# Squares of three norms' last tiles added by GpSimd instead of by products with ones, and a table load one instruction later

## The chip, the cores and the metric

The kernel runs on one core of a Trainium2 chip. Its time is device time in microseconds (us), the median of several executions. The engines are TensorE (PE, matrix products; PEld is its weight load), VectorE (DVE), ScalarE (ACT), GpSimd (POOL) and SyncE (SP, which issues the weight DMAs). Each engine runs its own instructions in order, and they wait for each other on counting semaphores.

## What is computed

Two layers of a first transformer block, then one layer of a second one, over 512 tokens and 1024 features. Each sublayer's result goes through an RMS norm before it is added to the residual stream `x`:

```python
def rms_norm(x, gain):
    xf = x.astype(jnp.float32)
    y = xf * lax.rsqrt(jnp.mean(xf * xf, axis=-1, keepdims=True) + RMS_EPS)
    return (y * gain.astype(jnp.float32)).astype(x.dtype)
...
        x = x + rms_norm_2(merged @ w_out[l], g_mix_post[l])
        h = rms_norm_2(x, g_mem_pre[l])
        m = rms_norm_2(mem, g_mem_kv[l])
```

What the change touches is the mean of squares over the 1024 features of three such values: the output projection (`wout`, once in each of the three layers), the gate of the per-layer embedding (`ple`, once in each of the two layers of the first block), and the memory (`mem`, 256 rows, once, in the second block).

## The kernel before

**Layout.** Features lie on the 128 partitions, in 8 tiles of 128 features; tokens lie along a row. So a sum of squares over the features is a sum over tiles and over partitions. The sum over partitions is a product with a matrix of ones on PE: `square_sum` (line 805) and `sum_of` (line 833) multiply a 256-token half of a tile of squares by `ones`, and several such products into one PSUM region also add tiles up. ACT then takes the root (`half_root`, lines 1511 to 1516: a logarithm and an exponential), DVE scales the tile into `sg`, POOL adds `sg` to `x` (line 3107), ACT and DVE split the new `x` into a rounded high and a low part (`h_hi`, `h_lo`, or `raw_x_hi`, `raw_x_lo` for the next layer), and PE multiplies these.

**Order of the sublayer.** Projections of 8 output tiles run tiles 0 to 3 over all 512 tokens, and then `last_units` (line 1079): the last four tiles, two at a time in one PSUM bank, first for tokens 0 to 255 (units 4 and 5 of the count, half 0) and then for tokens 256 to 511 (units 6 and 7, half 1). Between units, each engine's order is written out by hand. PE goes from half 1 of `wout` straight on to the next stage's first products (`first_units`, line 1100), which start on half 0 of the new `x`; from half 1 of `ple` it goes to `begin` (line 860). The norm's whole chain for half 0 has to be done beside PE's products of half 1, and the chain for half 1 beside PE's first products of the next stage.

**Who adds the squares.** ACT squares tiles 0 to 3 into `sq`, POOL adds them into `sq_acc` (a part of the tile `rstd`; line 3102). ACT squares units 4 to 7 too (`half_squares` line 1518, `ple_squares` line 1956). Of each half POOL adds only the first unit (two instructions of 128x256, line 3068); the second unit's two squares go to PE as they are. So each half of `wout` costs PE 3 products (1 of `sq_acc`, 2 of `sq`), half 0 of `ple` 3, and half 1 of `ple` 5 (two more of `res`, where the last unit's squares of that half lie). The memory's 8 squares go to PE one product each (`sum_mem`, lines 1316 to 1319), two behind each of the tiles 4, 6, 8 and 10 of the merge `am`. PE's place for a sum is fixed: behind the second block (k or j = 1) of the unit that follows, for `ple` behind j = 6 (half 0) and k = 5 (half 1).

**DVE beside it.** When ACT has squared a unit, DVE copies it out of PSUM (`half_out`, line 2272). In `wout`, what follows on DVE behind unit 5 is the low part of a weight unit (`w_lo`, `gu_lo` or `mq_lo`, line 2132), and behind unit 7 the tree of additions for the next norm (lines 2265 and 2266). In `ple`, what follows behind unit 7 is line 2132 and then the tree of lines 2190 and 2191.

Of the kernel before, what the change touches and what calls it, by code (L numbers as in the profile page):

```python
# [176 lines left out]
def stage(name, A=0, **more):  # L177
# [16 lines left out]
    stage("wout", A=8, SS=6, AD=7), stage("post1", N=2, X=16),  # L194
    stage("norm2", W=16, SQ=16, Q=2, SS=4, N=2), stage("gu", A=KF, R=KF, G=KF),
    stage("dn", A=8, SS=2, AD=6), stage("post2", N=1, X=8),
    stage("pp"), stage("xple", W=8), stage("ple", A=8, SQ=8, SS=2, AD=5), stage("post3", N=2, X=16),
# [5 lines left out]
    stage("bm2", A=8), stage("am", A=8), stage("normm", R=8, SQ=8, SS=8, N=1),  # L203
    stage("mk"), stage("mv"), stage("dsa", I=32, H=16, O=4), stage("cm", A=8, R=8),
    stage("wout", A=8, SS=6, AD=7), stage("post1", N=2, X=16),
# [74 lines left out]
def block_kernel(nc, stream, xT, pT, memT, vec1, gains, cst, pos, out):  # L280
    with ExitStack() as ctx:
# [418 lines left out]
        def _(pe):  # L700
# [123 lines left out]
            def half_sum(c, st, half):  # L824

                if st == "mo":
                    direct_sum(c, st, half)
                    return
                square_sum(sq_added, c.at("AD", st, 5 + 2 * half), sq_acc[:, cols(half)], True, False, ps=HALF_SS[half])
                for j in range(2):  # L830
                    square_sum(act_took, c.at("A", st, 6 + 2 * half), sq[:, j, cols(half)], False, j == 1, ps=HALF_SS[half])
# [7 lines left out]
            def gate_sum(c, half):  # L839

                pe.wait_ge(sq_added, c.at("AD", "ple", 5))
                pe.wait_ge(sq_ready, c.at("SQ", "ple", 6 + 2 * half))
                last = [sq[:, j, cols(half)] for j in range(2)]
                if half == 1:
                    last += [res[:, 0, cols(j)] for j in range(2)]
                sum_of([sq_acc[:, cols(half)]] + last, half)
# [13 lines left out]
            def begin(c, st, turn):  # L860
# [27 lines left out]
                for half in range(2):  # L888
                    at = cols(half)
                    for i, p in enumerate(in_turn(half)):  # L890
                        if half == 0:
                            pe.wait_ge(lo_ready, c.at("U", st, p + 1))
                        ps = free_bank(c, st, 2 * half + i)
                        hi, lo = home(c, u0 + p)
                        for k in range(KD):
                            if i == 0:
                                pe.wait_ge(raw_split, c.begun("W", KD * half + k + 1))
                            for g in range(2):
                                b = slice((8 * g + k) * P, (8 * g + k + 1) * P)
# [200 lines left out]
            def first_units(c, st, norm_st, before, also=None):  # L1100

                u0 = c.base[st]["U"]
                for half in range(2):
                    at = cols(half)
                    for p in range(2):
# [4 lines left out]
                        for k in range(KD):  # L1110
# [6 lines left out]
                            if half == 0 and p == 0 and k == (KD - 1 if before == "mo" else 1):  # L1117
                                half_sum(c, before, 1)
# [48 lines left out]
            def first_block(L):  # L1167
# [115 lines left out]
                last_units(c, "ple", lambda k, at: h_hi[:, k, at], lambda k, at: h_lo[:, k, at], 6)  # L1283
# [106 lines left out]
        def _(act):  # L1390
# [127 lines left out]
            def half_squares(c, st, n):  # L1518
# [3 lines left out]
                act.wait_ge(sq_added, c.at("AD", st, 3 + two * (2 + 2 * half)))  # L1522
# [83 lines left out]
            def project_norm(c, st, after, which, norm_st):  # L1606
# [14 lines left out]
                half_root(c, st, 0, 3, HALF_RSTD[0][:, 0:HALF])  # L1621
# [5 lines left out]
                half_root(c, st, 1, 6, HALF_RSTD[1][:, 0:HALF])  # L1627
# [209 lines left out]
            def first_block(L):  # L1837
# [127 lines left out]
                ple_gate(5)  # L1965
                log_table()
                ple_squares(5)
# [103 lines left out]
            def norm_mem(m):  # L2071

                if 1 <= m <= 4:
                    for j in range(2 * m - 2, 2 * m):
                        squares(c, "normm", j, memf[:, j, :], (mem_loaded, 16), N_MEM)
                elif m == 5:
                    root("normm", c, KD, N_MEM, D, dst=mem_rstd[:, :])
# [937 lines left out]
        def _(pool):  # L3015
# [47 lines left out]
            def half_squares(c, st, half, ready=act_took, kind="A"):  # L3063

                for j in range(2):
                    pool.wait_ge(ready, c.at(kind, st, 5 + 2 * half))
                    pool.wait_ge(sq_added, c.at("AD", st, 3 + j + 2 * half))
# [28 lines left out]
            def project_norm(c, st, after, ready=act_took, kind="A"):  # L3096
# [361 lines left out]
```

## Time and profile before

| | |
|---|---|
| time, 3 runs | 2672.48 us median (2671.38 to 2672.74) |
| the profiled execution | 2670.99 us, span of its trace 2668.9 us |
| granted TensorE clock | 0.998 of full speed |
| PE busy | 2622.5 us, 98% of the span |
| DVE, ACT, POOL busy | 1720.7, 1310.8, 494.9 us |
| weight load on PE busy | 2268.1 us |
| DMA | 246.55 MB, mean 92 GB/s |

PE is busy nearly all the time, and the other engines have time left; DMA is far from full. Busy time is an average, though. What matters for this change is what each engine does in some twenty stretches of about 5 us, and which of the waits there is the last. A matmul's record is longer than its turn, since matmuls are pipelined: turns are read from start to start.

### The profile page before, as it was taken

The numbers are of one execution on the slowest core, as the hardware profiler recorded it, in microseconds if no ns is written. First come the engines' busy times: TensorE is split into PE (matmuls) and PEld (weight loads), VectorE is DVE, ScalarE is ACT, GpSimd is POOL, SyncE is SP. The second block draws the span as 40 slices with busy tenths as digits, with TensorE's granted clock in tenths as the row PEclk, the third lists the DMA queues.
The fourth block names the chain that finished last, engine by engine and source line by source line (L and its number), as shares of the span: only waits on it lengthen the run. The fifth ranks groups of instructions, "written<-read, shape, count | busy, mean of one in ns | idle before, by whom it ended". The sixth has DMA issues, their size and how long they took to land.

```text
span 2668.9 us, 40629 instructions
## 1 busy us (share of the span) xinstructions
PE 2622.5 (98%) x15848; PEld 2268.1 (85%) x15848; DVE 1720.7 (64%) x2770; ACT 1310.8 (49%) x2297; POOL 494.9 (19%) x515
## 2 busy tenths in 40 slices
PE   8999999999999999999999999999999999999997
PEld 7887778999988988777899998897787689999986
DVE  6767544888624765755389872475689536798743
ACT  6446543555524644654355562463634635555531
POOL 1424001210102311500121010241011012210101
PEclk9999999999999999999999999999999999999999
DMA  4321123223332232111222233222232221123232
GB/s 153 126 95 36 53 79 112 76 89 105 112 110 95 80 127 95 48 56 64 95 94 84 109 111 111 95 95 79 95 111 80 83 101 69 64 95 110 103 120 79
DMA packets 37958, 246.55 MB, mean 92 GB/s; under 512 B 4624, under 2 KB 5648, under 8 KB 8976
## 3 DMA queue, kind: packets, MB, share of 16 engines
q1 hardware_dynamic: 34032, 239.09, 25.3%
q10 hardware_dynamic: 3744, 4.94, 0.5%
q8 instruction: 126, 2.06, 0.3%
q14 instruction: 56, 0.46, 0.1%
HBM read 241.91 MB, written 2.10 MB: 91 GB/s over the span
## 4 chain that ended last, share of the span: by engine, by line
PE 55%; DVE 2%; issue 1%; ACT 1%; POOL 0%; ACTq 0%; POOLq 0%
PE bank L711 13%; PE bank L713 12%; PE bank L712 12%; PE bank L1159 4%; PE bank L1161 4%; PE bank L1160 4%; PE bank L992 1%; PE bank L949 1%; PE bank L808 1%; PE bank L1304 0%; PE bank L970 0%; PE bank L921 0%; ACT w_hi L1415 0%; DVE st_neg L2436 0%; PE bank L1005 0%
## 5 line engine op out<-in xcount | busy, mean ns | idle before, releaser
L2132 DVE TENSOR_TENSOR w_lo<-raw,w_hi 128x2048 fp32r<-128x2048 f32 x129 | 300.4, 2329 | 322.6 <-ACT w_hi L1415 322.1
L711 PE MATMUL bank<-h_hi,w_hi 128*128 128x512 f32 (+1 forms) x1224 | 474.0, 387 | 3.2 <-DVE ob_lo L2698 1.3
L713 PE MATMUL bank<-h_hi,w_lo 128*128 128x512 f32 (+1 forms) x1224 | 464.3, 379 | 0.0
L712 PE MATMUL bank<-h_lo,w_hi 128*128 128x512 f32 (+1 forms) x1224 | 463.7, 379 | 0.0
L1415 ACT ACTIVATE w_hi<-raw 128x2048 fp32r<-128x2048 f32 x148 | 282.3, 1910 | 223.4 <-PE bank L713 213.9
L1159 PE MATMUL bank<-half_hi,w_hi 128*128 128x256 f32 x1344 | 381.0, 283 | 0.0
L1161 PE MATMUL bank<-half_hi,w_lo 128*128 128x256 f32 x1344 | 380.8, 283 | 0.0
L1160 PE MATMUL bank<-half_lo,w_hi 128*128 128x256 f32 x1344 | 380.8, 283 | 0.0
L711 PEld LDWEIGHTS bank<-h_hi,w_hi 128*128 128x128 f32 x1224 | 230.5, 188 | 55.1 <-issue 11.9
L713 PEld LDWEIGHTS bank<-h_hi,w_lo 128*128 128x128 f32 x1224 | 230.4, 188 | 44.0
L712 PEld LDWEIGHTS bank<-h_lo,w_hi 128*128 128x128 f32 x1224 | 230.8, 189 | 39.3
L1159 PEld LDWEIGHTS bank<-half_hi,w_hi 128*128 128x128 f32 x1344 | 258.4, 192 | 0.1
L1160 PEld LDWEIGHTS bank<-half_lo,w_hi 128*128 128x128 f32 x1344 | 258.3, 192 | 0.1
L1161 PEld LDWEIGHTS bank<-half_hi,w_lo 128*128 128x128 f32 x1344 | 258.4, 192 | 0.0
L711 PE MATMUL bank<-a_hi,w_hi 128*128 128x512 f32 x528 | 205.9, 390 | 0.9 <-DVE w_lo L2144 0.9
L712 PE MATMUL bank<-a_lo,w_hi 128*128 128x512 f32 x528 | 205.6, 389 | 0.0
L713 PE MATMUL bank<-a_hi,w_lo 128*128 128x512 f32 x528 | 205.6, 389 | 0.0
L2531 DVE TENSOR_TENSOR w_lo<-raw,w_hi 128x512 fp32r<-128x512 f32 x192 | 141.5, 738 | 32.5 <-ACT w_hi L1726 31.3
L1669 ACT ACTIVATE pT<-bank 128x512 f32<-128x512 f32 (+3 forms) x160 | 79.7, 498 | 109.5 <-PE bank L949 109.4
L1726 ACT ACTIVATE w_hi<-raw 128x512 fp32r<-128x512 f32 x192 | 118.6, 623 | 17.5 <-PE bank L1161 9.3
L1789 ACT ACTIVATE parts<-bank 128x256 f32<-128x256 f32 x192 | 72.7, 378 | 94.7 <-PE bank L1161 94.6
L711 PEld LDWEIGHTS bank<-a_hi,w_hi 128*128 128x128 f32 x528 | 99.2, 188 | 21.8 <-DVE w_lo L2144 1.5
(510 smaller groups left out, 5749.4 us busy)
## 6 DMA issues: line engine op xcount, KB each, us to landing
raw<-in_stream SPq DMA_DIRECT2D x225, 1024.0 KB, 4.8
x<-in_xT SPq DMA_DIRECT2D x4, 512.0 KB, 9.2
out_T<-x ACTq DMA_DIRECT2D x8, 256.0 KB, 2.1
raw<-in_stream SPq DMA_DIRECT2D x2, 512.0 KB, 7.1
p_f<-in_pT ACTq DMA_DIRECT2D x2, 512.0 KB, 3.6
memf<-in_memT ACTq DMA_DIRECT2D x1, 1024.0 KB, 5.3
cst_sb<-in_cst ACTq DMA_DIRECT2D x1, 409.0 KB, 7.2
pos_i<-in_pos ACTq DMA_DIRECT2D x1, 258.0 KB, 5.4
```

The costliest lines, as they stand in the source:

```text
L711: nc.tensor.matmul(ps, wh, xh, start=start, stop=False)
L712: nc.tensor.matmul(ps, wh, xl, start=False, stop=False)
L713: return nc.tensor.matmul(ps, wl, xh, start=False, stop=stop)
L1159: nc.tensor.matmul(ps, wh[:, b], half_hi[:, i, k, :], start=opens, stop=False, skip_group_check=on)
L1160: nc.tensor.matmul(ps, wh[:, b], half_lo[:, i, k, :], start=False, stop=False, skip_group_check=on)
L1161: mm = nc.tensor.matmul(ps, wl[:, b], half_hi[:, i, k, :], start=False, stop=k == KD // 2 - 1, skip_group_check=on)
L1415: nc.scalar.activation(home(c, v)[0][:, :], raw[v % 2][:, :], ACT.Copy).then_inc(hi_ready, 1)
L1669: nc.scalar.activation(a["pT"][h % 2][:, 0:n, b * P:(b + 1) * P], turned_bank(c, st, i)[:, 0:n * P].rearrange("p (t q) -> p t q", t=n), AC ...
L1726: ins = nc.scalar.activation(factor(c, v, i, w_hi), factor_value(c, v, i), ACT.Copy)
L1789: nc.scalar.activation(parts[:, PIECES[i], :], ps[:, 0:HALF], ACT.Copy).then_inc(piece_taken, 1)
L2132: nc.vector.tensor_tensor(lo[:, :], raw[v % 2][:, :], hi[:, :].bitcast(F32), ALU.subtract).then_inc(lo_ready, 1)
L2531: ins = nc.vector.tensor_tensor(factor(c, v, i, w_lo), factor_value(c, v, i), factor(c, v, i, w_hi).bitcast(F32), ALU.subtract)
```

## The change

It does six things.

- **Units 5 and 7 of `wout`, and unit 5 of `ple`:** their two squares are now added into `sq_acc` by POOL, two more instructions each. Unit 6 of `ple` was in the sum of half 1 as `sq`; POOL adds it now. PE's sum is then one product for each half of `wout` and for half 0 of `ple`, and three for half 1 of `ple`.
- **Places on PE:** the sum of half 0 of `wout` stands behind block 6 instead of 1, that of half 1 behind block 3 instead of 1; in `ple` behind 7 instead of 6 and behind 6 instead of 5.
- **Waits:** each sum waits for POOL's additions alone (half 1 of `ple` also for ACT's last squares).
- **Places on POOL:** the two additions of unit 7 of `wout`, and those of unit 6 of `ple`, stand behind all eight additions to `x` of half 0 and ahead of those of half 1.
- **Table load:** in `ple`, ACT loads the logarithm's table behind the squares of unit 5, not ahead of them.
- **Memory norm:** ACT squares two tiles in one instruction (4 of 128x512 for 8 of 128x256), POOL adds them up (3 of 128x512, 1 of 128x256), and PE makes one product behind tile 10 for eight.

The core of the diff:

```diff
@@ half_sum, on PE
-                square_sum(sq_added, c.at("AD", st, 5 + 2 * half), sq_acc[:, cols(half)], True, False, ps=HALF_SS[half])
-                for j in range(2):
-                    square_sum(act_took, c.at("A", st, 6 + 2 * half), sq[:, j, cols(half)], False, j == 1, ps=HALF_SS[half])
+                square_sum(sq_added, c.at("AD", st, 7 + 4 * half), sq_acc[:, cols(half)], True, True, ps=HALF_SS[half])
@@ gate_sum, on PE
-                pe.wait_ge(sq_added, c.at("AD", "ple", 5))
-                pe.wait_ge(sq_ready, c.at("SQ", "ple", 6 + 2 * half))
-                last = [sq[:, j, cols(half)] for j in range(2)]
+                pe.wait_ge(sq_added, c.at("AD", "ple", 7 + 2 * half))
                 if half == 1:
-                    last += [res[:, 0, cols(j)] for j in range(2)]
-                sum_of([sq_acc[:, cols(half)]] + last, half)
+                    pe.wait_ge(sq_ready, c.at("SQ", "ple", 8))
+                sum_of([sq_acc[:, cols(half)]] + ([res[:, 0, cols(j)] for j in range(2)] if half == 1 else []), half)
@@ places on PE: begin, project, first_units, the gate
-                            if (half, i, k) == (0, 0, 5):
+                            if (half, i, k) == (0, 0, 6):
                                 gate_sum(Counts(BASE1, turn - 1), 1)
...
-                last_units(c, st, hi, lo, 1)
+                last_units(c, st, hi, lo, 6)
...
-                            if half == 0 and p == 0 and k == (KD - 1 if before == "mo" else 1):
+                            if half == 0 and p == 0 and k == (KD - 1 if before == "mo" else 3):
                                 half_sum(c, before, 1)
...
-                last_units(c, "ple", lambda k, at: h_hi[:, k, at], lambda k, at: h_lo[:, k, at], 6)
+                last_units(c, "ple", lambda k, at: h_hi[:, k, at], lambda k, at: h_lo[:, k, at], 7)
@@ sum_mem, on PE
-                for j in range(n - 4, n - 2) if n in (4, 6, 8, 10) else ():
-                    square_sum(sq_ready, c.at("SQ", "normm", j + 1), sq[:, j % 2, 0:N_MEM], j == 0, j == KD - 1)
+                if n == 10:
+                    square_sum(sq_added, c.at("AD", "normm", 4), sq[:, 0, 0:N_MEM], True, True)
@@ the gate, on ACT
                 ple_gate(5)
+                ple_squares(5)
                 log_table()
-                ple_squares(5)
@@ POOL, the norm behind wout and ple
-                half_squares(c, st, 0, ready, kind)
+                half_squares(c, st, 4, 3, ready, kind)
+                half_squares(c, st, 5, 5, ready, kind)
                 for half in range(2):
                     for m in range(KD):
                         pool.wait_ge(post_ready, c.at("X", after, KD * half + m + 1))
                         nc.gpsimd.tensor_tensor(x[:, m, cols(half)], x[:, m, cols(half)], sg[:, m % 2, cols(half)], ALU.add).then_inc(x_ready, 1)
                         if half == 0 and m == 4 and st != "ple":
-                            half_squares(c, st, 1)
+                            half_squares(c, st, 6, 7)
+                    if half == 0 and st == "ple":
+                        half_squares(c, st, 6, 7, ready, kind)
+                    elif half == 0:
+                        half_squares(c, st, 7, 9)
@@ POOL, ahead of norm(c, "normm", 2)
+            for j in range(1, 4):
+                pool.wait_ge(sq_ready, c.at("SQ", "normm", j + 1))
+                if j >= 2:
+                    pool.wait_ge(sq_added, c.at("AD", "normm", j - 1))
+                nc.gpsimd.tensor_tensor(sq[:, 0, :], sq[:, 0, :], sq[:, 1, :], ALU.add).then_inc(sq_added, 1)
+            pool.wait_ge(sq_added, c.at("AD", "normm", 3))
+            nc.gpsimd.tensor_tensor(sq[:, 0, 0:N_MEM], sq[:, 0, 0:N_MEM], sq[:, 0, N_MEM:S], ALU.add).then_inc(sq_added, 1)
```

The order of instructions, which stands in the program and holds no times: first POOL in the norm behind the first layer's `wout`, before. L3102 adds the squares of tiles 0 to 3, L3068 those of the last units, L3107 adds to `x`, L3044 belongs to the feed-forward part.

```order
106 L3018 TENSOR_TENSOR m_lo_125<-res,m_hi_124 128x512 x8
107 L3102 TENSOR_TENSOR rstd<-sq 128x512
108 L3102 TENSOR_TENSOR rstd<-rstd,sq 128x512 x2
109 L3068 TENSOR_TENSOR rstd<-rstd,sq 128x256 x2
110 L3107 TENSOR_TENSOR x<-x,sg 128x256 x5
111 L3068 TENSOR_TENSOR rstd<-rstd,sq 128x256 x2
112 L3107 TENSOR_TENSOR x<-x,sg 128x256 x11
113 L3044 TENSOR_TENSOR a_lo_127<-res,a_hi_126 128x512 x4
```

The same stretch of POOL's order now (L3108 is the addition to `x`):

```order
106 L3017 TENSOR_TENSOR m_lo_125<-res,m_hi_124 128x512 x8
107 L3102 TENSOR_TENSOR rstd<-sq 128x512
108 L3102 TENSOR_TENSOR rstd<-rstd,sq 128x512 x2
109 L3068 TENSOR_TENSOR rstd<-rstd,sq 128x256 x4
110 L3108 TENSOR_TENSOR x<-x,sg 128x256 x5
111 L3068 TENSOR_TENSOR rstd<-rstd,sq 128x256 x2
112 L3108 TENSOR_TENSOR x<-x,sg 128x256 x3
113 L3068 TENSOR_TENSOR rstd<-rstd,sq 128x256 x2
114 L3108 TENSOR_TENSOR x<-x,sg 128x256 x8
```

Four additions of squares stand ahead of the additions to `x` where two stood, and two more stand between those of half 0 and those of half 1.

Second, ACT at the gate of the first layer, before. `res<-bank` takes unit 5 out of PSUM, `sq<-e` squares it, L1515 and L1516 are the root of half 0.

```order
633 L1956 ACTIVATE sq<-e 128x2x256
634 L1436 ACTIVATE res<-bank 128x512
635 L1460 ACT_TABLE_LOAD
636 L1956 ACTIVATE sq<-e 128x2x256
637 L1515 ACTIVATE rstd<-bank 128x256
```

And now (L1456 is the table load, L1952 the squares):

```order
633 L1952 ACTIVATE sq<-e 128x2x256
634 L1432 ACTIVATE res<-bank 128x512
635 L1952 ACTIVATE sq<-e 128x2x256
636 L1456 ACT_TABLE_LOAD
637 L1511 ACTIVATE rstd<-bank 128x256
```

The squares of unit 5 and the table load have changed places; nothing else moved on ACT here. DVE's order is the same before and now over the whole program.

## Rows read from the trace of the kernel before

**Rows 1.** what PE waited for: us in total, times, longest us

```profile
PE bank L711 <- DVE raw_x_lo L2658: 10.9, 1, 10.9
```

**Rows 2.** timeline of PE, first `wout`, half 0: start, us, instruction [idle before <-releaser]

```profile
462.68 0.28 PE L713 MATMUL bank<-m_hi,w_lo 128*128 128x256 f32 x1
462.80 0.60 PE L808 MATMUL bank<-rstd,cst_sb 128*128 128x256 f32 x2
...
464.21 0.28 PE L712 MATMUL bank<-m_lo,w_hi 128*128 128x256 f32 x1
```

**Rows 3.** timeline of PE, first gate, the sums of half 0 and half 1

```profile
875.73 0.28 PE L713 MATMUL bank<-h_hi,w_lo 128*128 128x256 f32 x1
876.28 0.67 PE L836 MATMUL bank<-rstd,cst_sb 128*128 128x256 f32 x2 [0.27 <-ACT sq L1956]
...
877.77 0.28 PE L712 MATMUL bank<-h_lo,w_hi 128*128 128x256 f32 x1
...
890.84 0.28 PE L713 MATMUL bank<-raw_x_hi,second_lo 128*128 128x256 f32 x1
...
893.32 0.28 PE L712 MATMUL bank<-raw_x_lo,second_hi 128*128 128x256 f32 x1
```

**Rows 4.** one line of POOL: duration ns min/median/max, first and last start

```profile
L3068 POOL TENSOR_TENSOR rstd<-rstd,sq x16: 727/782/2327, 457.3 to 2225.0; 128x256 f32<-128x256 f32 x16
```

**Rows 5.** timeline, GpSimd and VectorE at the first gate and ahead of the first `dn`

```profile
869.42 2.29 DVE L2132 TENSOR_TENSOR second_lo<-raw,second_hi 128x2048 fp32r<-128x2048 f32 x1 [1.11 <-ACT second_hi L1415]
...
869.98 2.33 POOL L3068 TENSOR_TENSOR rstd<-rstd,sq 128x256 f32<-128x256 f32 x1 [5.38 <-ACT sq L1956]
...
714.33 5.50 DVE L2481 TENSOR_TENSOR a_lo<-a_val,a_hi 128x512 fp32r<-128x512 f32 x9
720.59 3.65 DVE L2132 TENSOR_TENSOR w_lo<-raw,w_hi 128x2048 fp32r<-128x2048 f32 x1 [0.75 <-ACT w_hi L1415]
...
717.40 4.69 POOL L3210 TENSOR_TENSOR p_lo<-p_f,p_hi 128x1024 fp32r<-128x1024 f32 x1 [10.60 <-ACT p_hi L1929]
```

**Rows 6.** timeline of the first `wout`, half 0, unit 5

```profile
462.34 0.60 ACT L1524 ACTIVATE sq<-bank 128x512 f32<-128x512 f32 x1
464.30 0.39 ACT L1515 ACTIVATE rstd<-bank 128x256 f32<-128x256 f32 x1 [1.36 <-PE bank L808]
...
463.58 2.28 DVE L2132 TENSOR_TENSOR gu_lo<-raw,gu_hi 128x2048 fp32r<-128x2048 f32 x1
```

**Rows 7.** timeline of the same norm, half 1, unit 7

```profile
475.29 0.48 DVE L2258 SCALAR_TENSOR_TENSOR h_lo<-x,vec,h_hi 128x256 fp32r<-128x256 f32 x1 [0.30 <-ACT h_hi L1532]
...
476.68 1.22 DVE L2265 TENSOR_TENSOR sq<-sq 128x1024 f32<-128x1024 f32 x1
...
475.47 0.57 ACT L1524 ACTIVATE sq<-bank 128x512 f32<-128x512 f32 x1
...
476.33 0.60 PE L808 MATMUL bank<-rstd,cst_sb 128*128 128x256 f32 x2
```

**Rows 8.** timeline of the first gate: VectorE in half 0, then half 1, unit 6

```profile
878.69 0.87 DVE L2823 SCALAR_TENSOR_TENSOR sg<-e,vec,bank 128x256 f32<-128x256 f32 x2 [3.77 <-ACT bank L1516]
...
889.13 0.62 ACT L1956 ACTIVATE sq<-e 128x512 f32<-128x512 f32 x1
...
890.08 2.28 DVE L2132 TENSOR_TENSOR w_lo<-raw,w_hi 128x2048 fp32r<-128x2048 f32 x1
892.28 1.21 DVE L2190 TENSOR_TENSOR sq_x<-sq_x 128x1024 f32<-128x1024 f32 x1
```

**Rows 9.** timeline of the memory norm: ACT's last squares, PE's last two products

```profile
2024.88 0.41 ACT L1456 ACTIVATE sq<-memf 128x256 f32<-128x256 f32 x1
...
2033.15 1.02 PE L808 MATMUL bank<-sq,cst_sb 128*128 128x256 f32 x4
```

**Rows 10.** timeline behind the third `wout`: VectorE's first query tile, PE's first score

```profile
2242.54 1.41 DVE L2280 SCALAR_TENSOR_TENSOR mq<-bank,rstd 128x256 f32<-128x256 f32 x4
...
2244.39 0.38 PE L1005 MATMUL bank<-mk,mq 128*128 128x256 f32 x1
```

More of the change, by code:

```diff
@@ L193 @@
     stage("am", A=8), stage("cm", A=8, R=8),
-    stage("wout", A=8, SS=6, AD=7), stage("post1", N=2, X=16),
+    stage("wout", A=8, SS=2, AD=11), stage("post1", N=2, X=16),
     stage("norm2", W=16, SQ=16, Q=2, SS=4, N=2), stage("gu", A=KF, R=KF, G=KF),
     stage("dn", A=8, SS=2, AD=6), stage("post2", N=1, X=8),
-    stage("pp"), stage("xple", W=8), stage("ple", A=8, SQ=8, SS=2, AD=5), stage("post3", N=2, X=16),
+    stage("pp"), stage("xple", W=8), stage("ple", A=8, SQ=8, SS=2, AD=9), stage("post3", N=2, X=16),
     stage("begin", W=16),
@@ L202 @@
     stage("z2", A=9, R=8), stage("lru", A=4, R=4),
-    stage("bm2", A=8), stage("am", A=8), stage("normm", R=8, SQ=8, SS=8, N=1),
+    stage("bm2", A=8), stage("am", A=8), stage("normm", R=8, SQ=4, SS=1, AD=4, N=1),
     stage("mk"), stage("mv"), stage("dsa", I=32, H=16, O=4), stage("cm", A=8, R=8),
-    stage("wout", A=8, SS=6, AD=7), stage("post1", N=2, X=16),
+    stage("wout", A=8, SS=2, AD=11), stage("post1", N=2, X=16),
     stage("normh", W=16, SQ=16, Q=2, SS=4, N=2), stage("mq"), stage("mem", I=16, H=4, O=4),
@@ L1521, in half_squares @@
                 dst = sq[:, :, cols(half)]
-                act.wait_ge(sq_added, c.at("AD", st, 3 + two * (2 + 2 * half)))
+                act.wait_ge(sq_added, c.at("AD", st, 3 + two * (2 + 4 * half)))
                 act.wait_ge(tile_done, c.at("T", st, n + 1))
@@ L1620, in project_norm @@
                 half_squares(c, st, 5)
-                half_root(c, st, 0, 3, HALF_RSTD[0][:, 0:HALF])
+                half_root(c, st, 0, 1, HALF_RSTD[0][:, 0:HALF])
                 for m in range(KD):
@@ L1626, in project_norm @@
                 half_squares(c, st, 7)
-                half_root(c, st, 1, 6, HALF_RSTD[1][:, 0:HALF])
+                half_root(c, st, 1, 2, HALF_RSTD[1][:, 0:HALF])
                 last_half(c, norm_st, which, after, "gu" if norm_st == "norm2" else "mq")
@@ L2073, in norm_mem @@
                 if 1 <= m <= 4:
-                    for j in range(2 * m - 2, 2 * m):
-                        squares(c, "normm", j, memf[:, j, :], (mem_loaded, 16), N_MEM)
+                    act.wait_ge(mem_loaded, 16)
+                    if m >= 3:
+                        act.wait_ge(sq_added, c.at("AD", "normm", m - 2))
+                    nc.scalar.activation(sq[:, min(m - 1, 1), :].rearrange("p (j t) -> p j t", j=2), memf[:, 2 * m - 2:2 * m, :],
+                                         ACT.Square).then_inc(sq_ready, 1)
                 elif m == 5:
-                    root("normm", c, KD, N_MEM, D, dst=mem_rstd[:, :])
+                    root("normm", c, 1, N_MEM, D, dst=mem_rstd[:, :])
                 elif m == 6:
@@ L3061, in add_squares, with half_squares @@
                     nc.gpsimd.tensor_tensor(sq_acc, sq[:, 0, :] if j == 1 else sq_acc, sq[:, j % 2, :], ALU.add).then_inc(sq_added, 1)
-            def half_squares(c, st, half, ready=act_took, kind="A"):
+            def half_squares(c, st, n, at, ready=act_took, kind="A"):
+                half = (n - 4) // 2
                 for j in range(2):
-                    pool.wait_ge(ready, c.at(kind, st, 5 + 2 * half))
-                    pool.wait_ge(sq_added, c.at("AD", st, 3 + j + 2 * half))
+                    pool.wait_ge(ready, c.at(kind, st, n + 1))
+                    pool.wait_ge(sq_added, c.at("AD", st, at + j))
                     nc.gpsimd.tensor_tensor(sq_acc[:, cols(half)], sq_acc[:, cols(half)], sq[:, j, cols(half)], ALU.add).then_inc(sq_added, 1)
```

## The prediction

> **What bounds the kernel now.** I read the page's busy times first: PE works 98% of the span, 2622.5 of 2668.9 us. Then the list of what PE waited for: the longest entry is one wait of 10.9 us at the program's start, and no other reaches 3 us in total [rows 1]. So PE's queue is the path nearly everywhere. A product taken from it shortens the kernel by its turn, and a stall put into it lengthens the kernel by the stall. Everything below is therefore a sum over PE's queue, place by place, made from the timelines of the stretches in question. DVE, ACT and POOL count only where PE's sum has to wait for them.
>
> **What one product with ones costs.** In the first `wout` the last ordinary product ahead of the sum starts at 462.68 and the sum at 462.80, so an ordinary turn of 256 columns is 0.12 us. Without the sum the next L712 would start at 462.92; it starts at 464.21 [rows 2]. Three products cost 1.29 us, 0.43 each. At the gate, L712 would start at 875.97 and starts at 877.77: 1.80 us, of which 1.29 is the three products and the rest a wait for ACT's squares. Half 1's five products cost 893.32 less 891.08, 2.24 us [rows 3].
>
> **What is removed.** Three times in `wout` 4 products, twice in the gate 4, in the memory norm 7: 27 products, 11.6 us. That is the gain if no sum waits.
>
> **What is added on POOL.** One addition of 128x256 takes 0.73 to 0.78 us undisturbed, but one took 2.33 [rows 4]. The timeline shows why [rows 5]. That add began at 869.98, in the middle of DVE's L2132 (869.42 to 871.71), and ended at 872.31, 0.6 us behind DVE's end, as if it had stood still until then. `p_lo` on POOL began at 717.40 during a run of nine two-input DVE instructions, which went on undisturbed until 719.83, and took 4.69 us; the L2132 that DVE began at 720.59, while POOL was still in it, took 3.65 instead of 2.29. So a POOL addition and a DVE instruction with two inputs in SBUF do not run side by side: one stands until the other is through. A DVE instruction that waits gets its turn when POOL's current instruction ends, and a row of ready DVE instructions keeps POOL out. What decides the change is which DVE instruction stands beside each new pair of additions.
>
> **`wout`, half 0 (three times).** ACT's squares of unit 5 end at 462.94 [rows 6]. POOL's first add runs from about 463.02 to 463.80. DVE's L2132 asks at 463.58, waits, and goes next: its 2.28 us end at about 466.0. The second add must follow the first and ends 0.6 us later, 466.6. PE reaches its new place five blocks of 3 x 0.12 us behind the old one, at 464.60. It stalls 2.05 us, then makes one product: 2.05 + 0.43 - 1.29 = **+1.2 us**. If the second add got in ahead of L2132, the data would be there at 464.65: -0.8. The other two layers' timelines have the same order and distances. I take +1.2, since every row with DVE waiting has it go next. The root follows: the old one began 1.50 us behind the sum's start [rows 6], with one product 0.64 us, so 467.3, and its two steps of 0.4 end at 468.1. DVE's `sg`, ready so far at L2132's end (465.86), is 2.3 us late.
>
> **`wout`, half 1 (three times).** The chain of half 0 carries those 2.3 us to ACT's squares of unit 7: 476.04 [rows 7] becomes 478.34. POOL's first add runs to 479.2; DVE's copy out of PSUM is beside it, then comes L2265 (1.22 us), which takes the turn to about 480.3; the second add ends at 480.95. PE's place, two blocks of 0.72 us on and 1.2 us late, is reached at 476.33 + 1.44 + 1.2 = 479.0. Stall 2.0, one product 0.43, less 1.29: **+1.15 us**. The chain behind it is now 3.8 us late. For the next products' low parts that is covered: half 0's last, done at 475.77 [rows 7], is 2.3 us late and is wanted at 474.89 + 1.2 + 7 x 0.72 = 481 (476.33 less two blocks is 474.89); half 1's has more room. Behind the third `wout` it is not: DVE's query tiles follow its tree without a gap and end at 2243.95, PE's first score starts at 2244.39 [rows 10]. One moves by 3.8, the other by 2.3: **+1.1 us**.
>
> **Gate, half 0 (twice).** The squares move ahead of the table load: DVE's idle time of 3.77 us up to 878.69 [rows 8] puts the end of its last step at 874.92, so ACT's squares end at about 875.6, where so far they ended just ahead of PE's start at 876.28 [rows 3]. DVE is idle then, so the two adds take 1.6 us and end at 877.25. PE arrives at 876.21, stalls 1.04 and pays 0.43, against 1.80 before: **-0.3 us**. The table load lies in that wait and costs nothing; without this cover it would be 1.3 us.
>
> **Gate, half 1 (twice).** Unit 6's squares end at 889.75 [rows 8], 0.2 later now, so POOL asks at 889.95. DVE is then in its last two-input instruction ahead of L2132; L2132 and L2190 follow it without a gap, from 890.08 to 893.5 [rows 8]. By the `p_lo` row they keep POOL out; the adds end at about 894.1 and, with one DVE instruction between, 895.2. PE's place is 891.35 (890.96 + 0.72 - 0.33). Stall 3.9, then three products for 1.4, against 2.24: **+3.0 us**.
>
> **Memory norm (once).** ACT's last squares end near 2025.6, PE's sum has its place at 2033.15 [rows 9]; POOL has 7.5 us for two adds, of 128x512 and 128x256, and by twice and once the 0.78 us of [rows 4] they take 2.3. Seven products go: **-3.0 us**. ACT's wider squares save under a microsecond beside PE.
>
> **A rule beside a row.** The p_lo row shows POOL waiting through several DVE instructions that were issued after it. The Trainium skill ("SBUF — State Buffer", "Who interferes with whom") says that issue order decides who blocks, and that the winner holds the shared ports for its whole instruction. By that rule POOL, which asks at 889.95, would go ahead of L2132: that is the second rival below, while for `wout` rule and rows give one result, since L2132 asks before the second add.
>
> **Sum.** Three times (1.2 + 1.15), and 1.1: 8.15. Twice (3.0 - 0.3): 5.4. Less 3.0. That is +10.5 us on the profiled execution's 2670.99, or 2681.5. The median of the runs lies 1.5 above it: **2683.0 us**.
>
> **Rivals.**
> 1. The adds don't collide, the side where it is faster. If POOL's adds ran at 0.83 us whatever DVE does, half 0 of `wout` would give -0.8, half 1 +0.35 (squares end at 476.4, adds at 478.15, place at 476.9), the gate -0.3 and -0.8, the memory norm -3.0: -6.6 us, 2665.9. It decides from the point at which the second add of a pair ends within 0.1 us of PE's place. Against it stand the 2.33, 4.69 and 3.65 us of [rows 4, 5]; for it, that the file has no pair with DVE asking in its middle. Chance 0.12.
> 2. POOL gets its turn ahead of L2132 at the gate. First add done at 890.9, L2132 until 893.1, second add 893.7, stall 2.35: +1.45 instead of +3.0, so 2679.9. Chance 0.2.
> 3. POOL's second add wins in `wout`, half 0. Then half 0 gives -0.8, half 1 +1.2, the queries nothing: 2676 with the gate as forecast, 2673 with rival 2 as well. Chance 0.15.
> 4. DVE keeps its turn through L2266 and the tree at the gate as well, 0.7 us at each of five places, and the late chains eat into the next stage's operands: 2687 or more. Chance 0.08.
> The forecast has 0.45.
>
> **How the numbers follow.** About 0.2% of the time, 5.3 us, is what a measurement of this kernel can tell from no change: faster is below 2667.1, slower above 2677.8. Forecast, rival 2 and rival 4 are slower: 0.73. Rival 3 is within: 0.15. Rival 1 is faster: 0.12. The range takes in all but rival 1 and the far end of rival 4: 2673 to 2688.
>
> **What would show it.** In the changed profile, PE waits for POOL's L3068 at the sums of `wout` about 2 us each, six times, and at half 1 of the gate near 4 us, twice; today that list has none. The second add of unit 5 in `wout` should take over 2 us and end 0.6 us behind L2132. If both adds of each pair take under 0.9 us, the forecast is wrong and rival 1 right. If L2132 at the gate is stretched by an add ahead of it, it is rival 2; if L2132 in `wout` is late by two adds, rival 3. The gain of 3 us should stand by itself in the stretch of the memory norm.

## The result and the profile after

| | before | after |
|---|---|---|
| median of 6 runs each | 2672.09 us (2671.34 to 2672.74) | 2686.64 us (2685.48 to 2687.45) |
| ratio, with its 95% interval | | 1.0055 [1.0045, 1.0065] |
| profiled execution, span | 2670.99, 2668.9 us | 2687.45, 2685.6 us |
| granted TensorE clock | 0.998 | 0.995 |

The changed kernel is slower by 14.6 us, or 0.55%. The direction is as forecast, and the time lies in the range, 3.6 us above the forecast. The sum behind the forecast held in some terms and failed in others, and a cost that it did not contain is among the largest. One execution of the experiment e2 below ran at a granted clock of 0.855 and took 2861 us; e2's median leaves it out.

The busy times of the page first:

```profile
PE 2620.6 (98%) x15794; PEld 2263.8 (84%) x15794; DVE 1725.0 (64%) x2770; ACT 1310.6 (49%) x2293; POOL 526.3 (20%) x539
```

PE has 27 products less and is busy only 2 us less (2622.5 before), in a span 16.7 us longer: it waits more, and some of its products take longer. The list of PE's waits (us in total, times, longest us) now reads as follows. Of these the list before had the first [rows 1], and `w_lo` with 1.2 us in total and 0.6 at the longest:

```profile
PE bank L711 <- DVE raw_x_lo L2657: 11.1, 1, 11.1
PE bank L808 <- POOL rstd L3068: 9.4, 6, 1.8
PE bank L834 <- POOL rstd L3068: 6.2, 4, 2.1
PE bank L711 <- DVE w_lo L2131: 3.7, 3, 2.4
```

Rows 2 and 3 are the sums of `wout` and of the gate, which wait for POOL's additions. The one wait of 2.4 us for `w_lo` is at the memory norm.

**`wout`.** The timeline of the first layer's `wout`, half 0 and then half 1 (start, us, instruction, [idle before <-releaser]), which answers to [rows 2, 6, 7]:

```profile
462.40 0.58 ACT L1520 ACTIVATE sq<-bank 128x512 f32<-128x512 f32 x1
463.05 3.46 POOL L3068 TENSOR_TENSOR rstd<-rstd,sq 128x256 f32<-128x256 f32 x2 [3.86 <-ACT sq L1520]
463.62 2.32 DVE L2131 TENSOR_TENSOR gu_lo<-raw,gu_hi 128x2048 fp32r<-128x2048 f32 x1
466.57 0.70 PE L808 MATMUL bank<-rstd,cst_sb 128*128 128x256 f32 x2 [1.84 <-POOL rstd L3068]
467.30 0.38 ACT L1511 ACTIVATE rstd<-bank 128x256 f32<-128x256 f32 x1 [4.33 <-PE bank L808]
...
477.84 0.58 ACT L1520 ACTIVATE sq<-bank 128x512 f32<-128x512 f32 x1
478.49 2.40 POOL L3068 TENSOR_TENSOR rstd<-rstd,sq 128x256 f32<-128x256 f32 x2 [1.41 <-ACT sq L1520]
479.06 1.25 DVE L2264 TENSOR_TENSOR sq<-sq 128x1024 f32<-128x1024 f32 x1
480.94 0.70 PE L808 MATMUL bank<-rstd,cst_sb 128*128 128x256 f32 x2 [1.82 <-POOL rstd L3068]
```

POOL's two additions take 3.46 us together in half 0: 0.57 ahead of DVE's low part, the 2.32 of that part, and 0.57 behind its end. In half 1 the instruction between them is the tree's first (1.25 us), and they take 2.40.

**Gate, half 1**, which answers to [rows 8]. The additions start on the stretch that [rows 3] show as PE's:

```profile
893.68 0.68 DVE L2807 TENSOR_TENSOR e<-e,res 128x512 f32<-128x512 f32 x1
894.04 3.65 POOL L3068 TENSOR_TENSOR rstd<-rstd,sq 128x256 f32<-128x256 f32 x2 [1.63 <-ACT sq L1952]
894.29 2.83 DVE L2131 TENSOR_TENSOR w_lo<-raw,w_hi 128x2048 fp32r<-128x2048 f32 x1
897.04 1.74 DVE L2189 TENSOR_TENSOR sq_x<-sq_x 128x1024 f32<-128x1024 f32 x1
897.75 0.70 PE L834 MATMUL bank<-rstd,cst_sb 128*128 128x256 f32 x2 [2.08 <-POOL rstd L3068]
```

L2131 takes 2.83 us, 0.55 more than its 2.28: it waited for POOL's first addition, which went ahead of it. The second addition waited for L2131, and L2189, 1.74 instead of 1.21, for the second addition. They took turns.

**The memory norm**, which answers to [rows 9]:

```profile
2040.16 2.29 DVE L2131 TENSOR_TENSOR w_lo<-raw,w_hi 128x2048 fp32r<-128x2048 f32 x1
2042.51 0.79 PE L711 MATMUL bank<-h_hi,w_hi 128*128 128x512 f32 x1 [2.44 <-DVE w_lo L2131]
```

In the kernel before, the same low part and the products that use it stood like this:

```profile
2027.89 2.29 DVE L2132 TENSOR_TENSOR w_lo<-raw,w_hi 128x2048 fp32r<-128x2048 f32 x1
...
2030.39 0.40 PE L711 MATMUL bank<-h_hi,w_hi 128*128 128x512 f32 x1
```

DVE ended at 2030.18, and PE used it 0.2 us later: the seven products were all that kept PE from waiting there. DVE has nothing to spare in this stretch: it is busy 9.6 of the 10 us from 2020 on before, and 9.7 after. Its low part began 12.27 us later than before, exactly what PE had lost up to the stage ahead. Nothing of what was taken from PE reached it.

**The clock.** PE's busy time in stretches of 2 us (stretch, us, PE busy (instructions), granted clock, DMA share, GB/s), behind the wait of half 1 of the first `wout`:

```profile
480.00:482.00 2.00, 1.05 (x7) 1.00 0.04 8
482.00:484.00 2.00, 2.00 (x12) 0.55 0.00 0
484.00:486.00 2.00, 2.00 (x13) 0.59 0.00 0
486.00:488.00 2.00, 2.00 (x18) 1.00 0.00 0
```

For some 3.4 us the granted clock is at the lower of its two levels, 1.2 instead of 2.4 GHz (a slice that holds both shows a mean of the two; cut into slices of 0.2 us the stretch is 482.2 to 485.6), and PE does 25 products in 4 us where the slice behind does 18 in 2. There are five such stretches, behind 480.94, behind the gates' second halves, behind the second `wout`'s half 0 and at the wait of 2.44 us, where it begins 0.3 us ahead of the wait's end. The profiled execution before has none from 10 us on while PE works; at its end the clock falls near 2657, 2 us behind PE's last product.

Comparing the start of the same ordinary product in both traces gives the account, after less before. The last column is from traces of experiments in which the same place passed at full clock, `wout` 1 in e1, the gates in e2, the memory norm in e3; for `wout` 2 it is an estimate from the length of the stretch:

| stretch | forecast, us | measured, us | of it for the half clock, about |
|---|---|---|---|
| `wout` 1 | +2.35 | +3.9 | 1.5 |
| gate 1 | +2.7 | +2.85 | 1.5 |
| `wout` 2 | +2.35 | +2.65 | 1.5 |
| gate 2 | +2.7 | +2.8 | 1.5 |
| memory norm | -3.0 | +0.9 | 1.3 |
| `wout` 3 and the queries | +3.45 | +3.5 | 0 |
| sum | +10.5 | +16.6 | 7.3 |

### The profile page after: what moved, and what is told of

The parts are those of the page before. It is cut to its first block, busy times and chain, and to the rows that moved or that the text cites. A ratio compares the mean times of both kernels' runs of the same rounds, so it can differ in the third digit from the quotient of the medians.

```text
span 2685.6 us, 40557 instructions
## 1 busy us (share of the span) xinstructions
PE 2620.6 (98%) x15794; PEld 2263.8 (84%) x15794; DVE 1725.0 (64%) x2770; ACT 1310.6 (49%) x2293; POOL 526.3 (20%) x539
## 3 DMA queue, kind: packets, MB, share of 16 engines
q8 instruction: 126, 2.06, 0.3%
## 4 chain that ended last, share of the span: by engine, by line
PE 49%; DVE 5%; issue 2%; ACT 2%; POOL 2%; DMA 0%; ACTq 0%; SPq 0%; POOLq 0%; DVEq 0%
PE bank L711 11%; PE bank L712 11%; PE bank L713 11%; PE bank L1155 4%; PE bank L1157 4%; PE bank L1156 4%; PE bank L988 1%; PE bank L945 1%; POOL x L3108 1%; POOL rstd L3068 1%; DVE score L2904 1%; DVE top L2903 1%; ACT w_hi L1411 1%; PE bank L808 0%; PE bank L1300 0%
## 5 line engine op out<-in xcount | busy, mean ns | idle before, releaser
L2131 DVE TENSOR_TENSOR w_lo<-raw,w_hi 128x2048 fp32r<-128x2048 f32 x129 | 301.4, 2337 | 324.4 <-ACT w_hi L1411 323.9
```

Source lines behind the costliest of these rows:

```text
L2131: nc.vector.tensor_tensor(lo[:, :], raw[v % 2][:, :], hi[:, :].bitcast(F32), ALU.subtract).then_inc(lo_ready, 1)
```

## The experiments

All times are medians, and each is compared with runs of the kernel before on the same chip in the same hour. The differences in the text are of these medians.

| kernel | us | before | ratio [95%] |
|---|---|---|---|
| e1 `wout` alone | 2681.21 | 2671.30 | 1.0037 [1.0023, 1.0050] |
| e2 gate alone | 2675.60 | 2671.30 | 1.0014 [1.0004, 1.0023] |
| e3 memory norm alone | 2671.70 | 2671.30 | 1.0001 [0.9992, 1.0010] |
| e4 stalls filled | 2684.24 | 2671.30 | 1.0048 [1.0034, 1.0062] |
| e5 low part in quarters | 2682.39 | 2671.82 | 1.0037 [1.0023, 1.0051] |
| e6 one square each | 2669.45 | 2671.82 | 0.9992 [0.9983, 1.0001] |
| e7 table load back | 2686.68 | 2671.82 | 1.0057 [1.0043, 1.0071] |
| e8 late places | 2685.18 | 2671.82 | 1.0049 [1.0035, 1.0062] |
| e9 a wait alone | 2687.45 | 2671.50 | 1.0058 [1.0044, 1.0071] |
| e10 one each, earlier place | 2668.97 | 2671.50 | 0.9989 [0.9980, 0.9998] |

**The three parts alone (e1, e2, e3).** Each takes its part of the diff shown ahead of the prediction and leaves the other two as before: e1 `half_sum`, its places and POOL's additions for `wout`; e2 `gate_sum`, its places, POOL's additions for `ple` and the table load; e3 `sum_mem` with ACT's and POOL's part of it.

> The kernel before with the change's output projection part alone (12 products fewer, 12 additions on GpSimd more). Lock theory (each second addition stands behind a two-input VectorE instruction): PE stalls of about 1.8 us at six sums, +2.4 us for each of three projections, and +1.1 us for the first score behind the third one: +8.3 us; with a stretch of TensorE at half clock behind the stalls of two of the three, some 1.5 us each, up to +11.3. So 2680.5 to 2683.5. Rival (additions run beside VectorE, each product is a gain of 0.43 us): -5 us or less. Rival (the projection is harmless and the loss is the gate's): within 1 us of before.

> The kernel before with the change's gate part alone (8 products fewer, table load later). From the two traces: half 0 about 0 each, half 1 a stall of about 2.1 us for 0.86 us of products taken away, +1.2 each, and a stretch at half clock behind it, +1.7 each: about +5.7 us, 2678. If the half clock comes only where a projection's stalls went before, +2.4 us, 2674.5. Rival without a lock: -2.2 us, 2670.

> The kernel before with the memory norm's part alone (7 products fewer). My prediction's step: -3.0 us, 2669.1. New theory (VectorE is busy 96% of this stretch and sets the time; PE gets ahead by 2.6 us and then waits as long for the low part of a weight unit, and a stretch at half clock of 1.7 us follows, less the last 0.43): +0.9 us, 2673.0. Without the clock -0.7 us.

Measured: +9.9, +4.3 and +0.4 us, 14.6 together, as the whole change. The intervals of e1 to e3 are some 2.4 to 3.6 us to either side, so the parts add up as far as the medians can tell. The memory norm, from which the forecast took 3.0 us, gives next to nothing: -0.4 us by the starts in e3's trace, at full clock, and its interval leaves out -3.0. e3's trace has the same wait as the changed kernel's, without anything else moved:

```profile
PE bank L711 <- DVE w_lo L2135: 2.4, 1, 2.4
```

The same waits do not always bring the half clock. In e2's trace neither wait at a gate's half 1 (2.08 and 2.06 us) does, and the gates cost 1.35 and 1.3 us. That execution (2673.53) is the second fastest of e2's. Behind the first, which ends at 893.80 (stretch, us, PE busy, granted clock, DMA share, GB/s):

```profile
894.00:896.00 2.00, 2.00 (x13) 1.00 0.75 221
896.00:898.00 2.00, 2.00 (x19) 1.00 0.75 311
```

In e1's trace one of five waits of 1.78 to 1.88 us at the sums is followed by it, at the third `wout`; the first two `wout` cost 2.5 and 2.4 us. Some 2 us of that trace's loss lie where e1 changes nothing: 0.8 at a stretch of half clock near 2312, behind a wait that the kernel before has too, and 1.3 near 2395, where DVE and then ACT are later than before. e3's wait of 2.42 us is followed by none either. One trace of a kernel therefore tells the cost of a wait, but not how often the half clock follows.

**The stalls filled (e4).** The changed kernel, with products into a PSUM region that the sum then overwrites, put ahead of each sum. PE works while it would stand; whatever the sums wait for is as late as before.

```diff
+            def fill(half, n):
+                for _ in range(n):
+                    nc.tensor.matmul(HALF_SS[half][:, 0:HALF], ones, cst_sb[:, 0:HALF], start=True, stop=True)
@@ half_sum
+                fill(half, 4)
@@ gate_sum
+                fill(half, 2 if half == 0 else 5)
```

> The changed kernel with products with ones of a constant, whose result is overwritten, ahead of PE's waits at the sums: 4 at each half of the output projection, 2 and 5 at the gate's halves, 0.43 us each, so that PE works in most of the stall and takes no longer for it. Clock theory (the half clock follows from PE's idling in the stalls): four of the five stretches at half clock go, about 1.6 us each, and 2680 comes out. Rival (the stretches have another cause, or working in the stall doesn't help): 2686.6, or 0.5 us more, as the changed kernel.

Measured: 2684.24, 12.9 us above before where the change has 14.6. The stretches at half clock behind the sums are gone; of the changed kernel's five only the one behind the unfilled wait for `w_lo` is left. The same place as above, in e4:

```profile
480.00:482.00 2.00, 1.93 (x10) 1.00 0.00 0
482.00:484.00 2.00, 2.00 (x19) 1.00 0.00 0
```

The gain is smaller than expected. In the profiled execution, 3.0 us faster than the changed kernel's, the first `wout` gains 1.3 us by the starts and the gates 1.7 and 1.6, as expected. The second `wout` loses 1.5 instead. There a weight's DMA landed later, ACT's high part and then the squares of unit 5 behind it, and the sum of half 0 still waited 1.58 us behind its filling. And half 1, whose sum had waited only 0.35 us behind the half clock, now pays for its filling in full. All five executions of e4 have a mean granted clock of 0.997; the six of the changed kernel have 0.994 to 0.996.

**A wait alone (e9).** The kernel before, with one wait more and no addition moved:

```diff
@@ half_sum
+                if half == 0:
+                    pe.wait_ge(lo_ready, c.at("U", st, 6))
```

> The kernel before, with nothing moved and nothing left out; only PE's sum of half 0 of wout (three times) also waits until DVE has made the low part that stands behind unit 5 (in the profile of before that ends at 465.86, and the sum starts at 462.80). So PE stands 3.06 us at three places and POOL does nothing new. Theory A (a stall of about 2 us or more is followed by a stretch of TensorE at half clock, whatever caused the stall): 3 x 3.06 for the stalls and 1.5 behind each, +13.7 us, 2685.4, with granted clock 0.5 to 0.6 shown within 20 us behind each place. Theory B (the half clock comes from the new work beside PE, POOL's additions or ACT's squares, and not from standing): 3 x 3.06 = +9.2 us and the clock as in the kernel before, 2681.

Measured: 2687.45, +16.0 us. The profiled execution (2686.20) has two stretches at half clock, behind the first and second wait; behind the third (3.09 us) there is none. Around the first wait, in e9:

```profile
464.00:466.00 2.00, 0.00 (x0) 1.00 0.00 0
466.00:468.00 2.00, 1.29 (x4) 0.81 0.20 37
468.00:470.00 2.00, 2.00 (x8) 0.50 0.79 303
470.00:472.00 2.00, 2.00 (x17) 0.84 0.45 184
472.00:474.00 2.00, 2.00 (x19) 1.00 0.00 0
```

By the starts, `wout` 1 costs 4.8 us, `wout` 2 4.8 and `wout` 3 3.3. Theory A holds for two of three places: the standing is enough, POOL's additions are not needed for it. But not every such stall is followed by a stretch at half clock, as the theory had it. Another 1.2 us came at what was 2384 before, where a weight's DMA landed later than in the trace of before.

**The low part in quarters (e5).** DVE's instruction behind unit 5 of `wout` in four pieces:

```diff
-                    split_unit(c, st, 3)
+                    v = c.base[st]["U"] + 5
+                    dve.wait_ge(hi_ready, c.at("U", st, 6))
+                    hi, lo = home(c, v)
+                    for q in range(4):
+                        at = slice(q * UC // 4, (q + 1) * UC // 4)
+                        ins = nc.vector.tensor_tensor(lo[:, at], raw[v % 2][:, at], hi[:, at].bitcast(F32), ALU.subtract)
+                    ins.then_inc(lo_ready, 1)
```

> The changed kernel, but DVE makes the low part that stands behind unit 5 of wout (three times, once for each layer) in four instructions of 128x512 instead of one of 128x2048. Nothing is left out. Theory A (who asked first goes first, one instruction at a time): POOL's second addition waits for one quarter only and ends near 465.0 in the first layer, so PE's wait at the sum of half 0 falls from 1.84 us to about 0.4, the chain behind it (and so the wait at half 1) from 1.8 to about 0.5, and the half-clock stretches behind wout go with it: about -3 us for each of the three, -6 to -9 us, 2678 to 2681. Theory B (a row of ready DVE instructions keeps POOL out, as I read the p_lo row): the second addition still ends 0.6 us behind the last quarter, the waits stay at 1.8 us and the time is that of the changed kernel, 2685 to 2688, plus 0.2 us for the added instructions.

The timeline of the first `wout` in e5, half 0 and PE's sum of half 1:

```profile
463.62 1.88 POOL L3074 TENSOR_TENSOR rstd<-rstd,sq 128x256 f32<-128x256 f32 x2 [3.80 <-ACT sq L1520]
464.18 3.07 DVE L2346 TENSOR_TENSOR gu_lo<-raw,gu_hi 128x512 fp32r<-128x512 f32 x4
465.55 0.70 PE L808 MATMUL bank<-rstd,cst_sb 128*128 128x256 f32 x2 [0.20 <-POOL rstd L3074]
...
479.96 1.00 PE L808 MATMUL bank<-rstd,cst_sb 128*128 128x256 f32 x2 [1.85 <-POOL rstd L3074]
```

Theory A: the additions take 1.88 us instead of 3.46, so the second waited for one quarter, with three more ready behind it. DVE's four quarters take 3.07 us instead of 2.32, since one of them waited for the addition. The wait of half 0 falls from 1.84 to 0.20 (0.33 and 0.27 in the other layers), and half 0 turns from +1.2 to about -0.4. The median falls by 4.0 us against the changed kernel's 14.6 above before, and not by 6 to 9, because the wait of half 1 stays (1.85, 1.84 and 1.83): there the second addition is behind the tree, and PE comes earlier by what half 0 saved. The half clock, which theory A had going too, stays as well: it follows all three of these waits in e5's trace.

**The table load back (e7).** At the gate the table is loaded ahead of the squares of unit 5 again.

> The changed kernel with one part undone: at the gate the logarithm's table is loaded ahead of the squares of unit 5 again. Nothing is left out. My theory: the squares come 1.3 us later, so do both additions; DVE's L2132 is not beside them there, PE waits at the sum of half 0 about 1.6 us instead of 1.0 or more: +0.6 to +1.3 us at each of two gates, 2688 to 2689. Rival: the sum waits for something else there and the place of the table load is worth nothing, 2686.6.

The time does not tell the two apart: 2686.68. The rows do. The sum of half 0 waits 1.49 us instead of 1.00, at both gates:

```profile
881.57 0.70 PE L834 MATMUL bank<-rstd,cst_sb 128*128 128x256 f32 x2 [1.49 <-POOL rstd L3068]
```

So the place of the table load is worth 0.5 us for each gate, which is less than the executions of one kernel differ by.

**Later places (e8).** PE's places moved behind the end of the additions, the memory norm as before:

```diff
-                            if (half, i, k) == (0, 0, 6):
+                            if (half, i, k) == (0, 1, 3):
-                last_units(c, st, hi, lo, 6)
+                last_units(c, st, hi, lo, 12)
-                            if half == 0 and p == 0 and k == (KD - 1 if before == "mo" else 3):
+                            if half == 0 and KD * p + k == (KD - 1 if before == "mo" else KD):
-                last_units(c, "ple", lambda k, at: h_hi[:, k, at], lambda k, at: h_lo[:, k, at], 7)
+                last_units(c, "ple", lambda k, at: h_hi[:, k, at], lambda k, at: h_lo[:, k, at], 10)
```

> The changed kernel with PE's places for the sums moved behind the time at which POOL's additions end now (half 0 of wout behind block 12 instead of 6, half 1 behind the eighth block of the next stage instead of the third, half 0 of the gate behind 10 instead of 7, half 1 behind the twelfth instead of the seventh), and the memory norm as before. Nothing is left out. Theory A (the loss is PE standing at the sums, and the half clock behind it; that the norm's chain is later costs nothing while there is cover): no waits for L3068, no half clock, 19 products less: wout of the first two layers -1.7 us each, the gates -1.5 each, the third wout about +1.7 since its queries follow without cover; about -4.5 us against before, 2666 to 2668. Theory B (the chain has no room): PE waits for the next stage's high and low parts instead, 2675 or more.

Measured: 2685.18, so theory B. The sums wait for POOL only 0.39 us at each half 1 of `wout`, and PE waits elsewhere (us in total, times, longest us):

```profile
PE bank L711 <- DVE w_lo L2128: 4.9, 4, 1.9
PE bank L1001 <- DVE mq L2276: 4.5, 1, 4.5
PE bank L708 <- POOL h_lo L3014: 2.9, 2, 2.3
PE bank L711 <- POOL h_lo L3014: 2.3, 1, 2.3
```

The first is mainly the gate (1.86 and 1.85 us): DVE's `w_lo` is late by the addition ahead of it, and PE comes to it without the sum's delay. The second is the queries behind the third `wout`, late by the later sum. The others are low parts that POOL makes behind the late norm. The trace is that of the slowest of the five executions, 3.6 us above their median. The chain had little room at three kinds of places, and the loss moved there. Four of these waits have a stretch at half clock behind them or at their end (near 894, 922, 1778 and 2260), which theory A had at none.

**One square each (e6, e10).** POOL adds only the first of the two squares of units 5 and 7 of `wout` and of units 5 and 6 of the gate, which ends before DVE's long instruction asks; PE takes the other. The sum of half 0 of `wout` stands behind block 4 instead of 6, and the memory norm is as before. The core of the edit to the changed kernel:

```diff
@@ half_sum
+                sum_of([sq_acc[:, cols(half)], sq[:, 1, cols(half)]], half)
@@ half_squares, on POOL; both=False for units 5 and 7 of wout, 5 and 6 of the gate
-                for j in range(2):
+                for j in range(2 if both else 1):
@@ place of half 1 behind the third wout, e10 alone
-                            if half == 0 and p == 0 and k == (KD - 1 if before == "mo" else 3):
+                            if half == 0 and p == 0 and k == (KD - 1 if before == "mo" else 2 if norm_st == "normh" else 3):
```

> The changed kernel, but POOL adds only the first of the two squares of each last unit (units 5 and 7 of wout, 5 and 6 of the gate), PE takes the other as a product; places of the sums nearer to the old ones; the memory norm is as before; the table load stays behind the squares. Nothing is left out. Theory A (the loss comes from the second addition, which has to wait for a DVE instruction with two inputs): one addition fits ahead of it, each wout half saves one product of 0.43 us without a wait, half 0 of the gate about 0.75, half 1 of it 0.43: about -5 us against the kernel before, 2666 to 2667. Theory B (the first addition is already too late, or PE's queue isn't what sets the time at these places): no gain, 2671 or more, with waits for L3068 at the sums.

> The kernel in which POOL adds one square of each last unit and PE takes the other, with one place changed: behind the third wout the sum of half 1 stands behind the third block of the next stage instead of the fourth, 0.72 us earlier, because there the query tiles follow the norm without cover. Nothing is left out. Theory A (behind the third wout the norm's chain sets the time, so the loss of 1.15 us seen there at the queries is the lateness of the sum): 0.5 to 0.7 us less than with the later place, 2668.8 or about -2.7 to -3.0 us against the kernel before. Rival (the queries are late for another reason): no change, 2669.4.

e6: 2669.45, 2.4 us below before, at an interval that just touches 1. Most additions stand alone now (0.74 us at the median), the longest wait of a sum is 0.62 us, and by the starts `wout` saves 0.2 to 0.4 us for each half (at the second one, half 0 loses 0.4 by that wait) and each gate 0.8. Against it stand 1.15 us at the queries. e10 moves that one sum back by a block, and the queries' loss is 0.43. Its median, 2668.97, is 2.5 us below the kernel before, 0.9989 [0.9980, 0.9998]. The step from e6 to e10 is smaller than the medians can tell; the rows show it. e10 is the only version whose interval lies below 1. Both fall short of the 5 us that e6's expectation had. The queries stand against the saving, and both profiled executions have a stretch at half clock behind a wait of 1.7 us near 2300 which the kernel before has too, at full clock. It costs 0.8 us in e6 and 0.95 in e10.

## Why the prediction was right, and where it was not

**Right in the main: what bounds the kernel.** The forecast was a sum over PE's queue. At `wout` and the gates a wait there came out as time, and e1 to e3 add up to the whole. At the memory norm DVE was as much the bound as PE.

**Right: `wout`, half 0 and half 1.** The second addition was put at 466.6 and ended at 466.51; the root at 467.3, where it started; `sg` at 468.1, and it started at 468.14. The stalls were put at 2.05 and 2.0 and measured 1.84 and 1.82. Each half came out at +1.2 where the clock stayed. Squares of unit 7 at 478.34: they ended at 478.42. e5 confirms the cause, since cutting DVE's one instruction removes the stall of half 0.

**Right: the queries.** +1.1 forecast, +1.14 measured; DVE's `mq` row and PE's wait of 0.89 us for it stand as the step said. e10 moves it by the sum's place.

**Right in the main: gate, half 0.** The stall was put at 1.04 and is 1.00. The gain was put at 0.3 and is 0.1.

**Wrong: gate, half 1, the stall.** The step that failed is "By the `p_lo` row they keep POOL out". POOL's first addition went ahead of L2132, as rival 2 had it. The stall is 2.08 us, not 3.9, and without the clock's part the place costs 1.4 (in e2) instead of 3.0, twice; rival 2 had +1.45. The rule from the Trainium skill that stood beside that row ("SBUF — State Buffer", "Who interferes with whom": issue order decides who blocks, for a whole instruction) holds for this row and for e5's. By them both engines take turns, one instruction at a time, in the order in which they ask. Why `p_lo`, which took 4.69 us, had to stand through several instructions of DVE [rows 5] is not explained by this; it was not tried.

**Wrong: the memory norm.** The step is "Seven products go: -3.0 us". Additions and squares were in time, as it said, but the step did not ask what PE would reach next. DVE's `w_lo` ended 0.2 us ahead of PE's use of it, and DVE was busy 96% of this stretch. PE came up to 2.7 us earlier and stood 2.44. At full clock the part gives -0.4 us (the traces of e3, e5 and e7) instead of -3.0.

**Missing: the clock.** No term and no rival had it. Five stretches of 1.3 to 1.5 us each are some 7.3 us in the profiled execution, nearly half of its loss. Its other executions have much the same mean granted clock, 0.994 to 0.996.

**Why the total came out near.** On the profiled execution the sum said +10.5 and +16.5 was measured. The clock's 7.3 and the memory norm's 2.6 without its part of the clock were missing; the two gates were over-estimated by 2.7, and in the second `wout` PE at half clock came later to the sum of half 1 and hardly stalled there, which took off some 1.2. 10.5 + 7.3 + 2.6 - 2.7 - 1.2 = 16.5. On the median it looks nearer still, 3.6 us, since the changed kernel's profiled execution is 0.8 above its median, where the forecast put the median 1.5 above the profile. The direction rests on the `wout` terms, which the runs bear out. That the time came within 3.6 us is in good part luck: two wrong terms and one missing offset each other.

## What to carry to other kernels

Taking work from the engine that bounds the kernel is worth its time only up to the next operand that is just in time: look for the slack of the next few products on other engines, not only at the work moved. Here, moving small additions to POOL paid only where they ended before DVE started a long two-input instruction: one addition that fits gained a little, and two lost much more. Price a new stall of 2 us on TensorE at more than its length: here about half of such stalls cost some 1.5 us more.

## What the hardware showed that was not expected

**Short stalls can halve TensorE's clock.** In the changed kernel eight waits of 1.77 to 2.44 us stand at the changed places, and five of them were followed by about 3.4 us at 1.2 GHz, each costing 1.3 to 1.5 us. Over all traces of the changed kernel and the experiments, 19 of 35 waits of 1.58 to 2.44 us at the changed places or soon behind them were. In e9 two of three waits of about 3 us were, and in e8 the one of 4.5. A wait of 1.7 us near 2300, which every version has, was followed by such a stretch in seven of twelve traces (e1, e3, e5, e6, e7, e8 and e10) and not in that of before, the changed kernel, e2, e4 or e9. None of the shorter waits was, the eight of 1.00 and 1.49 us at half 0 of the gates among them. In some cases the stretch began up to 0.5 us ahead of the wait's end, in others up to 1.8 us behind it. So at these lengths it happens or not. The Trainium skill ("TensorE: Matmul & The Clock Gate", "Part 1: The HAM clock gate (the "warmup" mystery)") names two levels of the clock, 1.2 and 2.4 GHz, which the rows here agree with (granted clock 0.50 inside each such stretch and 1.00 outside). It also says that the gate's window does not start with the kernel, which would fit a stretch that comes and goes with the same wait; no run here shows that cause.

**A late DMA can move a sum.** In e4, e9 and e10 a weight that landed 1.1 to 1.5 us later than in the trace of before reached PE through ACT or DVE, at places where before had no wait. Single traces of one kernel can therefore differ by 1 us at a place that no edit touched.
